# A hybrid mLSTM / gated-DeltaNet layer: the order of a head's work in the mLSTM stage

## Chip, cores, metric

One core of a Trainium2 chip runs the whole program. The metric is device time in microseconds; lower is better. A run of the kernel is compared with runs of the kernel before on the same chip.

## What is computed

One layer of a decoder trunk, for a prompt of 1024 tokens and a group of 8 sequences of 8 sample tokens (1088 tokens in all), float32. All tokens go through one input projection `h @ w_in` (width 1024 in), whose columns feed an mLSTM branch with 4 heads, a gated DeltaNet branch with 8 heads, and gates. Then follow the output projections, a squared-ReLU MLP and a gated side input. The change concerns the mLSTM branch alone. Per head, q and k have 128 columns, v and the output gate 256:

```python
# per chunk; C (128x256) and n (128) are carried
s   = einsum('bhld,bhjd->bhlj', qx, kx) * dw
num = w_inter * einsum('bhld,bhde->bhle', qx, C) + einsum('bhlj,bhje->bhle', s, vx)
nq  = w_inter * einsum('bhld,bhd->bhl', qx, n) + sum(s, axis=-1)
h   = num / maximum(abs(nq), exp(-m_row))
C   = dec * C + einsum('bhl,bhld,bhle->bhde', wk, kx, vx)      # and n likewise
ha  = head_rms(h) * g_norm_a * sigmoid(o_a)
```

The kernel's chunk is 128 tokens: eight of the prompt, and a ninth that holds all 64 sample tokens, each sequence with a C and n of its own, which are read from memory and written back.

## The kernel before

The program runs in stages with a barrier between them: prologue, gates, delta (DeltaNet), mlstm, tail. In each stage every engine has its own program, in order; semaphores join them.

**Projections.** Weights come in slabs of 128 output columns (512 KB). SyncE loads a slab into the one raw buffer (`Weights.load`, L199), VectorE rounds it to the high part (`split_hi`, L209), GpSimd subtracts to get the remainder (`split_lo`, L214), TensorE multiplies in three passes over 8 k-tiles (`product`, L225). High parts and remainders have two buffers. So the load of a slab waits for the remainder of the one before it, and the high part of a slab waits until the products of the slab two before it are done. A slab's product is three groups over tokens (384, 384, 320), each of 24 matmuls into one PSUM bank. A head has six slabs: 0 K, 1 Q, 2 and 3 V, 4 and 5 the output gate. ScalarE copies a group out of its bank (`copy_out`).

**Banks.** `Banks` gives out PSUM banks in a fixed rotation. `claim` makes TensorE wait until the user before has released the bank; six banks serve projections and matrices, two the recurrence, sample states and output transposes.

**A head's other work.** `matrices`: for three thirds of three chunks each, K and V are transposed (L1402) and K·Q formed (L1413). VectorE scales and copies these out and multiplies K·Q by decays; the decays' exponents are made by nine VectorE instructions (L1517) from rows loaded per head, and exponentiated by ScalarE. `scan_all`: for each of eight chunks the state product (L1425), the numerator in two products (L1427, L1429); VectorE updates C (L1547), ScalarE copies the numerator out (L1495). Then the sample numerator (L1435, L1437) and eight sample-state products (L1442), each added to CS by VectorE (L1559) after CS was scaled as a whole (L1555). `finish` on VectorE squares and sums the numerators (L1567 to L1574), ScalarE makes the inverse norm, VectorE scales NUM (L1576), splits slab 2 of the next head, makes the gates (L1582). `outputs`: TensorE transposes NUM (L1451) in six groups of three; VectorE multiplies them with the gates into HT (L1588), which are the buffers V0 and V1.

**Order before.** TensorE: slabs 1 to 5, `matrices`, `scan_all`, slab 0 of the next head, `outputs`. SyncE: for the head before, `stores` (C and n of the prompt, C and n of the samples, both HT tiles to HA; then a wait until the four states have landed); then the decay rows and the new head's CS; then slabs 3, 4, 5 and slabs 0, 1, 2 of the next head. The n stores write single float32 elements. VectorE: splits of slabs 3, 4, 5 and of the next head's 0 and 1, the exponents and `matrices`, `scan_all`, `finish`. ScalarE waits for the HA stores of the head before ahead of its first copy of slab 2.

```python
def turn(h, nxt):                  # TensorE, L1454
    for j in range(1, NJ):
        for g in range(NG):
            group(h, j, g)
    matrices(h)
    scan_all(h)
    if nxt:
        for g in range(NG):
            group(h + 1, 0, g)
    outputs(h)
```

Of the kernel before, what the change touches and what calls it, by code (L numbers as in the profile page):

```python
# [30 lines left out]
NB, NS = 8, 8  # L31
T = SEQ + NB * NS
L = 128
# [43 lines left out]
def wait(eng, ev, turn, n):  # L77
    eng.wait_ge(ev.sem, ev.at(turn, n))
# [151 lines left out]
def build(nc, x_prompt, x_sample, p_prompt, p_sample, state_C, state_n, state_m, state_S, state_conv, g_mix, w_in,  # L230
# [38 lines left out]
    with ctx:  # L269
# [999 lines left out]
        def mlstm():  # L1269
            NJ = 6  # L1270
            E1 = DV_A + 1
            dense = [("dense", j, g) for j in range(NJ) for g in range(NG)]
            mats = [(n, t) for t in range(3) for n in ("kt", "va", "vb", "p")]
            scan = [(n, c) for c in range(NC) for n in ("c", "num")] + [("num", NC)] + [("cs", b) for b in range(NB)]
            turn_ = [(n, t) for t in range(3) for n in ("ta", "tb")]
            B = Banks(psum[0:6], dense + mats, sem, "a_main")
            SB = Banks(psum[6:8], scan + turn_, sem, "a_scan")
            with ExitStack() as st:
# [40 lines left out]
                with nc.Block() as block:  # L1319
                    @block.sync  # L1320
                    def _(sp):
# [4 lines left out]

                        def turn(h, later, nxt):
                            if later:
                                stores(h - 1)
                            for i, (dst, src) in enumerate(((ROW, ROWS_A[bass.ds(h, 1), 0]), (WIN, ROWS_A[bass.ds(h, 1), 1]),  # L1330
                                                            (DECS, DECS_A[bass.ds(h, 1)]))):
                                sp.dma_start(dst[:], src.to_broadcast([P, dst.shape[1]])).then_inc(s_row[i].sem, 16)
                            sp.dma_start(CS[:, :, 0:DV_A], state_C[0, :, bass.ds(h, 1)].rearrange("b a k v -> k (b a) v")).then_inc(s_cs.sem, 16)
                            sp.dma_start(CS[:, :, DV_A:E1], state_n[0, :, bass.ds(h, 1)].rearrange("b a k -> k b a")).then_inc(s_cs.sem, 16)
                            for j in range(3, NJ):
                                slab(h, j)
                            if nxt:
                                for j in range(3):
                                    slab(h + 1, j)
# [48 lines left out]
                    def _(pe):  # L1388
# [15 lines left out]

                        def matrices(h):
                            for t in range(3):
                                turned(h, ("kt", t), K, [("dense", 0, min(t, 2))])
                                turned(h, ("va", t), V0, [("dense", 2, t)])
                                turned(h, ("vb", t), V1, [("dense", 3, t)])
                                bank = B.claim(pe, h, ("p", t), ("dense", 1, t))  # L1410
                                for i in range(3):
                                    a = (3 * t + i) * L
                                    ins = pe.matmul(bank[:, i * L:i * L + L], K[:, a:a + L], Q[:, a:a + L], start=True, stop=True)  # L1413
                                B.filled(ins, ("p", t))

                        def scan_all(h):
                            for c in range(NC):
                                a = c * L
                                if c % 3 == 0:
                                    for n in ("kt", "va", "vb", "p"):  # L1420
                                        B.taken(pe, h, (n, c // 3))
                                if c == 1:
                                    wait(pe, qi, h, 1)
                                bank = SB.claim(pe, h, ("c", c))
                                SB.filled(pe.matmul(bank[:, 0:E1], KW[:, a:a + L], VT[:, c, :], start=True, stop=True), ("c", c))  # L1425
                                bank = SB.claim(pe, h, ("num", c), *([("c", c - 1)] if c else []))
                                ins = pe.matmul(bank[:, 0:E1], ST[:, a:a + L], VT[:, c, :], start=True, stop=(c == 0))  # L1427
                                if c:
                                    ins = pe.matmul(bank[:, 0:E1], Q[:, a:a + L], C[c % 2][:], start=False, stop=True)  # L1429
                                SB.filled(ins, ("num", c))  # L1430
                            a = NC * L
                            bank = SB.claim(pe, h, ("num", NC))
                            wait(pe, s_cs, h, 2)
                            wait(pe, qm, h, 1)
                            pe.matmul(bank[:, 0:E1], ST[:, a:a + L], VT[:, NC, :], start=True, stop=False)  # L1435
                            for b in range(NB):
                                ins = pe.matmul(bank[:, 0:E1], QM[:, P * b:P * b + P], CS[:, b, :], start=False, stop=(b == NB - 1))  # L1437
                            SB.filled(ins, ("num", NC))
                            wait(pe, vm, h, 1)
                            for b in range(NB):  # L1440
                                bank = SB.claim(pe, h, ("cs", b))
                                SB.filled(pe.matmul(bank[:, 0:E1], KW[:, a:a + L], VM[:, b, :], start=True, stop=True), ("cs", b))  # L1442
# [11 lines left out]
                        def turn(h, nxt):  # L1454
                            for j in range(1, NJ):
                                for g in range(NG):
                                    group(h, j, g)
                            matrices(h)
                            scan_all(h)
                            if nxt:  # L1460
                                for g in range(NG):
                                    group(h + 1, 0, g)
                            outputs(h)

                        for g in range(NG):
                            group(0, 0, g)
                        pe.wait_ge(s_init, 6)
# [5 lines left out]
                    def _(act):  # L1473
# [9 lines left out]

                        def turn(h, later):
                            for j in range(NJ):
                                for g in range(NG):
                                    if later and g == 0 and j == 2:
                                        wait(act, s_ha, h - 1, 2)
                                    copy_out(h, j, g)
                            for t in range(3):  # L1490
                                wait(act, dx, h, t + 1)
                                act.activation(third(ST, t), third(ST, t), ACT.Exp).then_inc(dw.sem, 1)
                            for c in range(NCH):
                                src = SB.read(act, h, ("num", c))
                                SB.release(act.activation(NUM[:, c, :], src[:, 0:E1], ACT.Copy), ("num", c))  # L1495

                            wait(act, fin, h, NL - 1)
                            act.activation(rr[:], rr[:], ACT.Ln).then_inc(lnr.sem, 1)
                            wait(act, lnr, h, 1)
                            act.activation(rr[:], rr[:], ACT.Exp, scale=-0.5).then_inc(lnr.sem, 1)  # L1500

                        turn(0, False)
                        with act.Fori(1, H_A) as h:
                            turn(h, True)

                    @block.vector
                    def _(dve):
                        def matrices(h):
                            dve.tensor_copy(HG[:].unsqueeze(1), GTA[:, bass.ds(h, 1)])
# [6 lines left out]
                            for c in range(NCH):  # L1516
                                ins = dve.scalar_tensor_tensor(ST[:, c * L:c * L + L], ROW[:, c * L:c * L + L], HG[:, 0, c:c + 1],  # L1517
                                                               (madd if c < NC else madds)[:], ALU.add, ALU.add)
                                if c % 3 == 2:
                                    ins.then_inc(dx.sem, 1)  # L1520
                            for t in range(3):
                                s = slice(3 * t, 3 * t + 3)
# [13 lines left out]

                        def scan_all(h, later):
                            wait(dve, s_row[2], h, 1)
# [11 lines left out]
                            for t in range(3):  # L1550
                                B.taken(dve, h, ("va", t))
                                B.taken(dve, h, ("vb", t))
                            dve.tensor_tensor(VM[:], over_chunks(VT[:, NC, :], NB), over_tokens(ohb[:], E1), ALU.mult).then_inc(vm.sem, 1)
                            SB.read(dve, h, ("num", NC))
                            dve.tensor_tensor(CS[:], CS[:], over_tokens(DECS[:, NC:16], E1), ALU.mult).then_inc(csd.sem, 1)  # L1555
# [34 lines left out]
                        def turn(h, later, nxt):  # L1590
                            for j in range(3, NJ):
                                WS.split_hi(dve, h, j, B)
                            if nxt:
                                WS.split_hi(dve, h + 1, 0, B)
                                WS.split_hi(dve, h + 1, 1, B)
                            matrices(h)
                            scan_all(h, later)
                            finish(h, nxt)
# [592 lines left out]
```

## Time and profile before

| | |
|---|---|
| Median of 3 runs | 3146.91 us (3145.77 to 3149.1) |
| Profiled execution: time, span | 3151.03 us, 3149.0 us |
| Busy: PE, PEld | 2774.0 us (88%), 2657.4 us (84%) |
| Busy: DVE, ACT, POOL | 1136.8 us (36%), 655.4 (21%), 686.0 (22%) |
| mlstm stage in the span | about 1165 to 1655 us |
| Weight-slab loads of the stage | 24, 512 KB each, 3.9 us to landing (median) |

Times in the views count from the start of the span. PE is TensorE's matmul side and PEld its weight loads; a float32 product appears as two matmuls ("x2"). A row's bracket gives the idle time of the engine ahead of the instruction and what ended it. PEclk is the granted TensorE clock, 1.00 being 2.4 GHz.

### The profile page before, as it was taken

The page shows a single profiled execution, that of the slowest core. Times are in us where ns is not written, and L with a number is a line of the kernel's source. Part 1 is how long each engine was busy: PE and PEld are TensorE (multiplying, and loading weights), DVE is VectorE, ACT ScalarE, POOL GpSimd, SP SyncE. Part 2 cuts the span into 40 slices and gives each one's busy share as a digit, 9 for nine tenths or more (in the row PEclk, how much of TensorE's full clock was granted, in tenths as well). Part 3 has the DMA queues.
Part 4 walks back from the last instruction along what each step waited for, and adds up shares of the span by engine and source line. Part 5 has one row for each costly group of instructions (what it writes and reads, how often), then busy time and mean ns, then how long its engine had stood idle before and what let it go on. Part 6 is the DMA issues. An engine that isn't in the chain of part 4 may idle for free. (4 is left out here: it accounts for less than half of the span.)

```text
span 3149.0 us, 41997 instructions
## 1 busy us (share of the span) xinstructions
PE 2774.0 (88%) x16879; PEld 2657.4 (84%) x16879; DVE 1136.8 (36%) x1791; ACT 655.4 (21%) x1308; POOL 686.0 (22%) x376
## 2 busy tenths in 40 slices
PE   4399889888898879889967998989999999999997
PEld 2388879788787869879857998989999999999987
DVE  2352452533524521442343122154413213223444
ACT  3243443443434421111110000001100001001122
POOL 1330230221202202011003122234211212112422
PEclk7699999999999989999988999999999999999999
DMA  3111111011011112423423121121111111111112
GB/s 118 40 27 51 56 36 49 21 57 56 28 50 50 34 28 76 78 35 83 78 25 107 47 90 43 44 90 47 41 48 41 44 45 41 47 41 41 57 34 75
DMA packets 237643, 165.10 MB, mean 52 GB/s; under 512 B 23755, under 2 KB 225035, under 8 KB 237487
## 3 DMA queue, kind: packets, MB, share of 16 engines
q1 hardware_dynamic: 237542, 163.64, 19.0%
q8 instruction: 77, 1.26, 0.2%
q14 instruction: 24, 0.20, 0.0%
HBM read 135.84 MB, written 27.76 MB: 52 GB/s over the span
## 5 line engine op out<-in xcount | busy, mean ns | idle before, releaser
L214 POOL TENSOR_TENSOR t_w_lo<-t_w_raw,t_w_hi 128x1024 fp32r<-128x1024 f32 x120 | 274.1, 2285 | 1027.3 <-DVE t_w_hi L209 1027.3
L225 PE MATMUL bank<-t_rhi,t_w_lo 128*128 128x384 f32 (+1 forms) x1344 | 444.0, 330 | 40.5 <-POOL t_w_lo L214 20.3
L225 PE MATMUL bank<-hlo,t_w_hi 128*128 128x384 f32 (+1 forms) x1440 | 467.7, 330 | 0.0
L225 PE MATMUL bank<-hhi,t_w_lo 128*128 128x384 f32 (+1 forms) x1344 | 444.1, 330 | 25.8 <-DVE hlo L2060 13.2
L225 PE MATMUL bank<-hhi,t_w_hi 128*128 128x384 f32 (+1 forms) x1344 | 443.7, 330 | 0.0
L225 PE MATMUL bank<-t_rhi,t_w_hi 128*128 128x384 f32 (+1 forms) x1344 | 442.2, 329 | 0.0
L225 PE MATMUL bank<-t_rlo,t_w_hi 128*128 128x384 f32 (+1 forms) x1344 | 442.1, 329 | 0.0
L225 PEld LDWEIGHTS bank<-t_rhi,t_w_lo 128*128 128x128 f32 x1344 | 255.6, 190 | 43.7 <-issue 31.4
L225 PEld LDWEIGHTS bank<-hhi,t_w_lo 128*128 128x128 f32 x1344 | 256.8, 191 | 27.2 <-issue 21.2
L225 PE MATMUL bank<-hhi,b_w_lo 128*128 128x384 f32 (+1 forms) x768 | 262.5, 342 | 16.8 <-POOL b_w_lo L214 12.0
L225 PEld LDWEIGHTS bank<-hlo,t_w_hi 128*128 128x128 f32 x1440 | 274.2, 191 | 0.0
L225 PEld LDWEIGHTS bank<-hhi,t_w_hi 128*128 128x128 f32 x1344 | 256.3, 191 | 0.0
L225 PEld LDWEIGHTS bank<-t_rlo,t_w_hi 128*128 128x128 f32 x1344 | 255.5, 190 | 0.2
L225 PEld LDWEIGHTS bank<-t_rhi,t_w_hi 128*128 128x128 f32 x1344 | 255.4, 190 | 0.0
L225 PE MATMUL bank<-hlo,b_w_hi 128*128 128x384 f32 (+1 forms) x768 | 255.0, 332 | 0.0
L225 PE MATMUL bank<-hhi,b_w_hi 128*128 128x384 f32 (+1 forms) x768 | 254.6, 331 | 0.0
L214 POOL TENSOR_TENSOR b_w_lo<-b_w_raw,b_w_hi 128x1024 fp32r<-128x1024 f32 x32 | 83.8, 2620 | 663.9 <-DVE b_w_hi L209 663.9
L225 PE MATMUL bank<-hhi,a_w_lo 128*128 128x384 f32 (+1 forms) x576 | 192.9, 335 | 11.9 <-POOL a_w_lo L214 11.9
L225 PE MATMUL bank<-hlo,a_w_hi 128*128 128x384 f32 (+1 forms) x576 | 191.4, 332 | 0.0
L225 PE MATMUL bank<-hhi,a_w_hi 128*128 128x384 f32 (+1 forms) x576 | 191.2, 332 | 0.0
L2033 DVE TENSOR_TENSOR t_x<-t_x,bank 128x384 f32<-128x384 f32 (+1 forms) x120 | 63.6, 531 | 339.5 <-PE bank L225 332.2
L1947 ACT ACTIVATE t_acc<-t_v 128x384 f32<-128x384 f32 (+1 forms) x96 | 48.6, 507 | 624.5 <-DVE t_v L2053 624.4
(350 smaller groups left out, 4345.5 us busy)
## 6 DMA issues: line engine op xcount, KB each, us to landing
b_w_raw<-in_w_in_dram SPq DMA_DIRECT2D x32, 512.0 KB, 3.9
t_w_raw<-in_w_up_dram SPq DMA_DIRECT2D x32, 512.0 KB, 3.8
t_w_raw<-in_w_down_dram SPq DMA_DIRECT2D x32, 512.0 KB, 4.0
a_w_raw<-in_w_in_dram SPq DMA_DIRECT2D x24, 512.0 KB, 3.9
t_w_raw<-in_w_in_dram SPq DMA_DIRECT2D x16, 512.0 KB, 3.6
b_gam<-ROWS_B SPq DMA_DIRECT2D x8, 576.0 KB, 4.1
b_eg<-ROWS_B SPq DMA_DIRECT2D x8, 576.0 KB, 5.8
b_kb<-ROWS_B SPq DMA_DIRECT2D x8, 576.0 KB, 6.8
```

The source lines that it names most:

```text
L214: pool.tensor_tensor(self.lo[j % 2][:, 0:kt, :], self.raw[j % self.rs][:, 0:kt, :], self.hi[j % 2][:, 0:kt, :], ALU.subtract).then_inc(sel ...
L225: ins = pe.matmul(out, a[:, k, :], b[:, k, :], start=(start and k == 0 and i == 0), stop=(stop and k == kt - 1 and i == 2))
L1947: act.activation(ACC[:, a:a + w], V[:, a:a + w], ACT.Square).then_inc(rsq.sem, 1)
L2033: B.release(dve.tensor_tensor(XM[:, m, a:a + w], XM[:, m, a:a + w], src[:, 0:w], ALU.add), ("dense", j, g))
```

## The change

TensorE's program is reordered. Slabs 2 and 3 come first in a head's turn; each group of slab 4 is followed by one third of the matrices, each group of slab 5 by two chunks of the recurrence. The next head's slab 0 has its groups between chunks 4-5 and 6-7, behind chunk 7, and behind the sample numerator. The sample states come in two halves with the first group of the next head's slab 1 between them; its other two groups stand ahead of `outputs`. The rotation of the six banks follows that order. ScalarE's copies follow it too. On VectorE the exponents come behind the split of slab 3, the split of the next head's slab 0 behind `matrices`, that of slab 1 inside `scan_all`. On SyncE the load of slab 3 stands ahead of the stores of the head before; slab 4 is now the first load behind them.

```diff
-            dense = [("dense", j, g) for j in range(NJ) for g in range(NG)]
-            mats = [(n, t) for t in range(3) for n in ("kt", "va", "vb", "p")]
+            main = [("dense", j, g) for j in range(4) for g in range(NG)]
+            for t in range(3):
+                main += [("dense", 4, t)] + [(n, t) for n in ("kt", "va", "vb", "p")]
+            main += [("dense", 5, g) for g in range(NG)]
...
-            B = Banks(psum[0:6], dense + mats, sem, "a_main")
+            B = Banks(psum[0:6], main, sem, "a_main")
...
                         def turn(h, later, nxt):
+                            slab(h, 3)
                             if later:
                                 stores(h - 1)
...
-                            for j in range(3, NJ):
+                            for j in range(4, NJ):
                                 slab(h, j)
...
                         def turn(h, nxt):
-                            for j in range(1, NJ):
+                            for j in range(2, 4):
                                 for g in range(NG):
                                     group(h, j, g)
-                            matrices(h)
-                            scan_all(h)
+                            for t in range(3):
+                                group(h, 4, t)
+                                matrices(h, t)
+                            for g in range(NG):
+                                group(h, 5, g)
+                                for c in range(2 * g, 2 * g + 2):
+                                    scan_chunk(h, c)
                             if nxt:
-                                for g in range(NG):
-                                    group(h + 1, 0, g)
+                                group(h + 1, 0, 0)
+                            for c in range(6, NC):
+                                scan_chunk(h, c)
+                            if nxt:
+                                group(h + 1, 0, 1)
+                            sample_out(h)
+                            if nxt:
+                                group(h + 1, 0, 2)
+                            for b0 in (0, NB // 2):
+                                sample_state(h, b0)
+                                if nxt and b0 == 0:
+                                    group(h + 1, 1, 0)
+                            if nxt:
+                                for g in range(1, NG):
+                                    group(h + 1, 1, g)
                             outputs(h)
 
-                        for g in range(NG):
-                            group(0, 0, g)
+                        for j in range(2):
+                            for g in range(NG):
+                                group(0, j, g)
...
                             dve.tensor_tensor(VM[:], over_chunks(VT[:, NC, :], NB), over_tokens(ohb[:], E1), ALU.mult).then_inc(vm.sem, 1)
+                            if nxt:
+                                WS.split_hi(dve, h + 1, 1, B)
                             SB.read(dve, h, ("num", NC))
...
                         def turn(h, later, nxt):
-                            for j in range(3, NJ):
+                            WS.split_hi(dve, h, 3, B)
+                            exponents(h)
+                            for j in range(4, NJ):
                                 WS.split_hi(dve, h, j, B)
+                            matrices(h)
                             if nxt:
                                 WS.split_hi(dve, h + 1, 0, B)
-                                WS.split_hi(dve, h + 1, 1, B)
-                            matrices(h)
-                            scan_all(h, later)
+                            scan_all(h, later, nxt)
                             finish(h, nxt)
```

Left out: `matrices` and `scan_all` of TensorE are cut into `matrices(h, t)`, `scan_chunk(h, c)`, `sample_out(h)` and `sample_state(h, b0)` with the same instructions in each; the first lines of VectorE's `matrices` become `exponents(h)`; ScalarE's `turn` copies groups and numerators in TensorE's new order, with slab 1's last group behind the inverse norm.

## Rows read from the trace of the kernel before

**Rows 1.** Windows of projections: length; busy us (count) of PE, PEld, DVE, ACT, POOL; PEclk; DMA share, GB/s
```profile
1176.01:1190.52 14.51, 14.51 (x73) 14.51 (x74) 0.69 (x1) 0.98 (x2) 3.69 (x7) 0.81 0.58 163
1190.52:1202.52 12.00, 12.00 (x75) 12.00 (x74) 0.69 (x1) 1.42 (x3) 2.40 (x1) 1.00 0.44 122
1304.71:1318.01 13.30, 13.30 (x74) 13.30 (x73) 0.71 (x2) 0.98 (x2) 0.00 (x0) 0.89 0.95 204
```

**Rows 2.** Windows of the matrices: the last head's, and the sum of four
```profile
1597.37:1602.33 4.96, 4.96 (x48) 4.96 (x46) 4.43 (x10) 1.67 (x4) 0.00 (x0) 1.00 0.01 3
sum 36.74, PE 25.67 PEld 24.64 DVE 35.10 ACT 7.69 POOL 7.04; mean PE 6.42 PEld 6.16 DVE 8.77 ACT 1.92 POOL 1.76
```

**Rows 3.** Timeline of PE, head 0: start, us, instruction, count, [idle before <-releaser]
```profile
1256.67 0.69 PE L1402 MATMUL bank<-ident,a_v 128*128 128x128 f32 x2 [3.69 <-DVE a_kw L1524]
...
1264.59 0.60 PE L1429 MATMUL bank<-a_c,a_q 128*128 128x257 f32 x2
1265.03 0.60 PE L1425 MATMUL bank<-a_vt,a_kw 128*128 128x257 f32 x2
...
1266.64 0.60 PE L1425 MATMUL bank<-a_vt,a_kw 128*128 128x257 f32 x2
...
1301.95 2.46 PE L1451 MATMUL bank<-ident,a_num 128*128 128x128 f32 x9 [4.27 <-DVE a_v L1588]
```

**Rows 4.** Windows of the recurrence: the sum of four heads
```profile
sum 55.83, PE 47.33 PEld 32.42 DVE 26.17 ACT 10.79 POOL 0.00; mean PE 11.83 PEld 8.11 DVE 6.54 ACT 2.70 POOL 0.00
```

**Rows 5.** Windows of head 0: sample states, next slab 0, outputs
```profile
1278.60:1284.83 6.23, 4.35 (x17) 2.38 (x16) 4.80 (x8) 1.67 (x2) 0.00 (x0) 1.00 0.00 0
1284.83:1296.86 12.03, 12.03 (x74) 12.00 (x73) 9.24 (x10) 2.46 (x5) 0.00 (x0) 1.00 0.87 82
1296.86:1304.71 7.85, 3.57 (x20) 2.73 (x18) 6.58 (x8) 0.44 (x1) 2.81 (x1) 0.75 0.14 25
```

**Rows 6.** Timeline of SyncE: first state store, n store, row load, slab 3
```profile
1285.39 0.37 SPq L1344 DMA_DIRECT2D out_dram<-a_c  x1
...
1286.96 0.53 SPq L1348 DMA_DIRECT2D out_dram<-a_cs  x1
...
1310.92 0.36 SPq L1332 DMA_DIRECT2D a_row<-ROWS_A  x1
...
1314.15 4.05 SPq L199 DMA_DIRECT2D a_w_raw<-in_w_in_dram  x1
```

**Rows 7.** DMA issues of three heads' ends: KB, us to landing (n store; slab 3)
```profile
a_w_raw<-in_w_in_dram SPq DMA_DIRECT2D x1, 512.0 KB, 9.2
...
out_dram<-a_cs SPq DMA_DIRECT2D x1, 4.0 KB, 23.8
...
out_dram<-a_cs SPq DMA_DIRECT2D x1, 4.0 KB, 21.5
...
out_dram<-a_cs SPq DMA_DIRECT2D x1, 4.0 KB, 26.0
```

**Rows 8.** Timeline of DVE, end of head 0
```profile
1283.57 0.86 DVE L1559 TENSOR_TENSOR a_cs<-a_cs,bank 128x257 f32<-128x257 f32 x2 [0.36 <-PE bank L1442]
1284.78 0.86 DVE L1559 TENSOR_TENSOR a_cs<-a_cs,bank 128x257 f32<-128x257 f32 x2 [0.36 <-PE bank L1442]
1285.56 2.55 DVE L1567 TENSOR_TENSOR a_sqn<-a_num 128x2304 f32<-128x2304 f32 x1
...
1293.40 2.56 DVE L1576 TENSOR_TENSOR a_num<-a_num,a_rr 128x2304 f32<-128x2304 f32 x1 [1.67 <-ACT a_rr L1500]
1297.13 0.69 DVE L209 CAST a_w_hi<-a_w_raw 128x1024 fp32r<-128x1024 f32 x1 [1.17 <-PE bank L225]
1297.74 3.56 DVE L1582 TENSOR_SCALAR a_o<-a_o,a_gh 128x1088 f32<-128x1088 f32 x2
```

**Rows 9.** Timeline of POOL: remainders of slabs 2 and 3 of head 1
```profile
1297.90 2.81 POOL L214 TENSOR_TENSOR a_w_lo<-a_w_raw,a_w_hi 128x1024 fp32r<-128x1024 f32 x1 [44.00 <-DVE a_w_hi L209]
1324.21 2.40 POOL L214 TENSOR_TENSOR a_w_lo<-a_w_raw,a_w_hi 128x1024 fp32r<-128x1024 f32 x1 [23.49 <-DVE a_w_hi L209]
```

More of the change, by code:

```diff
@@ L1403, in turned @@
                             B.filled(ins, slot)
[L1405 to L1430, printed above, removed]
+                        def matrices(h, t):
+                            turned(h, ("kt", t), K, [("dense", 0, min(t, 2))])
+                            turned(h, ("va", t), V0, [("dense", 2, t)])
+                            turned(h, ("vb", t), V1, [("dense", 3, t)])
+                            bank = B.claim(pe, h, ("p", t), ("dense", 1, t))
+                            for i in range(3):
+                                a = (3 * t + i) * L
+                                ins = pe.matmul(bank[:, i * L:i * L + L], K[:, a:a + L], Q[:, a:a + L], start=True, stop=True)
+                            B.filled(ins, ("p", t))
@@ new lines, in scan_chunk @@
+                        def scan_chunk(h, c):
+                            a = c * L
+                            if c % 3 == 0:
+                                for n in ("kt", "va", "vb", "p"):
+                                    B.taken(pe, h, (n, c // 3))
+                            if c == 1:
+                                wait(pe, qi, h, 1)
+                            bank = SB.claim(pe, h, ("c", c))
+                            SB.filled(pe.matmul(bank[:, 0:E1], KW[:, a:a + L], VT[:, c, :], start=True, stop=True), ("c", c))
+                            bank = SB.claim(pe, h, ("num", c), *([("c", c - 1)] if c else []))
+                            ins = pe.matmul(bank[:, 0:E1], ST[:, a:a + L], VT[:, c, :], start=True, stop=(c == 0))
+                            if c:
+                                ins = pe.matmul(bank[:, 0:E1], Q[:, a:a + L], C[c % 2][:], start=False, stop=True)
+                            SB.filled(ins, ("num", c))
@@ L1431, in scan_all, with sample_out @@
+                        def sample_out(h):
                             a = NC * L
@@ L1438, in scan_all, with sample_state @@
                             SB.filled(ins, ("num", NC))
+                        def sample_state(h, b0):
+                            a = NC * L
                             wait(pe, vm, h, 1)
-                            for b in range(NB):
+                            for b in range(b0, b0 + NB // 2):
                                 bank = SB.claim(pe, h, ("cs", b))
@@ L1482, in copy_out, with numerator, turn @@
                             B.release(ins, ("dense", j, g))
-                        def turn(h, later):
-                            for j in range(NJ):
+                        def numerator(h, c):
+                            src = SB.read(act, h, ("num", c))
+                            SB.release(act.activation(NUM[:, c, :], src[:, 0:E1], ACT.Copy), ("num", c))
+                        def turn(h, later, nxt):
+                            for j in range(2, 4):
                                 for g in range(NG):
@@ L1492, in turn @@
                                 act.activation(third(ST, t), third(ST, t), ACT.Exp).then_inc(dw.sem, 1)
-                            for c in range(NCH):
-                                src = SB.read(act, h, ("num", c))
-                                SB.release(act.activation(NUM[:, c, :], src[:, 0:E1], ACT.Copy), ("num", c))
+                            for g in range(NG):
+                                copy_out(h, 4, g)
+                            for g in range(NG):
+                                copy_out(h, 5, g)
+                                for c in range(2 * g, 2 * g + 2):
+                                    numerator(h, c)
+                            if nxt:
+                                copy_out(h + 1, 0, 0)
+                            for c in range(6, NC):
+                                numerator(h, c)
+                            if nxt:
+                                copy_out(h + 1, 0, 1)
+                            numerator(h, NC)
+                            if nxt:
+                                copy_out(h + 1, 0, 2)
+                                for g in range(2):
+                                    copy_out(h + 1, 1, g)
                             wait(act, fin, h, NL - 1)
@@ L1500, in turn, with exponents @@
                             act.activation(rr[:], rr[:], ACT.Exp, scale=-0.5).then_inc(lnr.sem, 1)
-                        turn(0, False)
-                        with act.Fori(1, H_A) as h:
-                            turn(h, True)
+                            if nxt:
+                                copy_out(h + 1, 1, 2)
+                        for j in range(2):
+                            for g in range(NG):
+                                copy_out(0, j, g)
+                        turn(0, False, True)
+                        with act.Fori(1, H_A - 1) as h:
+                            turn(h, True, True)
+                        turn(H_A - 1, True, False)
                     @block.vector
                     def _(dve):
-                        def matrices(h):
+                        def exponents(h):
                             dve.tensor_copy(HG[:].unsqueeze(1), GTA[:, bass.ds(h, 1)])
@@ L1520, in matrices @@
                                     ins.then_inc(dx.sem, 1)
+                        def matrices(h):
                             for t in range(3):
@@ L1535, in matrices, with scan_all @@
                             dve.tensor_copy(QM[:].rearrange("p (b x) -> p b x", x=P + NS)[:, :, 0:NS], sequences(Q)).then_inc(qm.sem, 1)
-                        def scan_all(h, later):
+                        def scan_all(h, later, nxt):
                             wait(dve, s_row[2], h, 1)
@@ L1553, in scan_all @@
                             dve.tensor_tensor(VM[:], over_chunks(VT[:, NC, :], NB), over_tokens(ohb[:], E1), ALU.mult).then_inc(vm.sem, 1)
+                            if nxt:
+                                WS.split_hi(dve, h + 1, 1, B)
                             SB.read(dve, h, ("num", NC))
```

## The prediction

> **What bounds the kernel now.** The page comes first, with the table above: TensorE (PE) is busy for most of the span, and nothing else for much over a third, so time moves only where the matrix engine waits, runs at half its clock, or is made to. Next come the stretches of the mLSTM stage. A head has six slabs of projections, 12.00 us each at full clock [rows 1], and behind slab 5 stand four pieces with little to cover their waits. (1) Transposes and K·Q products, "matrices": 36.74 us over four heads, of which the last, whose exponents were ready, takes 4.96 [rows 2]. The other three share 31.78: each has a wait of 3.69 for a VectorE (DVE) product [rows 3]. (2) The recurrence over eight chunks: 55.83 over four heads, TensorE modelled busy for 47.33 [rows 4]. (3) The sample states, 6.23 [rows 5] (first of three, within 0.1 of each other). (4) The outputs, 7.85 (first of three, likewise), at granted clock 0.75 (1.00 is 2.4 GHz, 0.5 is 1.2), with one wait of 4.27 for VectorE [rows 3, 5]. The reader should see that these are latencies between engines, not work.
>
> Then the quiet side, SyncE's program. It issues in order; its store routine ends in a wait until a head's states have landed, and the next head's row loads stand behind it. The stores begin at 1285.39, the row loads can only go at 1310.92 [rows 6], because the 4 KB store of n (4 bytes a packet) takes 23.8 us to land; 21.5 and 26.0 at the next heads [rows 7]. Today this hides behind three slabs.
>
> I call E the end of a head's last sample product (1284.83), H the moment at which NUM is scaled (1293.40 + 2.56 = 1295.96), O the end of the output transposes (1304.71) [rows 5, 8].
>
> **Part by part.** The instructions are the same in kind and number; order and bank rotation change.
>
> *Matrices.* Each third now has a slab-4 group in front, and the exponents are taken behind slab 3's split, long before. The nearest row is the last head's 4.96, with its exponents early. Saved: 31.78 − 3 × 4.96 = 16.9 us (bounds: 5.8, if a wait of 3.69 stays in each of three heads, to 16.9).
>
> *Recurrence.* A chunk takes 1.61 (1265.03 to 1266.64); a product without a wait takes 0.44 (1264.59 to 1265.03) [rows 3], so three make 1.31, and the 23 of a head 10.0. The other 0.3 is the wait for ScalarE's copy of the numerator before. Behind a projection group the first chunk of a pair does not pay it and the second does: 4 × 0.3 stay, and 0.3 at the first copy of C. That is 11.5 a head, and 12.1 in the last, where chunks 4 to 7 stand together. Saved: 55.83 − 3 × 11.5 − 12.1 = 9.2 (bounds 6 to 13).
>
> *Sample states.* CS is scaled under a group of the next head's slab 0 and no longer in TensorE's way. What is left is VectorE's pace of additions, 1.21 for two [rows 8], behind a first pair at 0.9: 2.1 for each half of four, 4.2 against 6.3. Saved three times: 6.3 (bounds 4 to 7.5).
>
> *Outputs.* Here cover is lost. H ends a chain on VectorE that begins 0.73 behind E: squares, sum, norms, scaling, to E+11.1 [rows 8]. Before, the 12.03 of slab 0 stood there [rows 5]; now only two groups of slab 1 (704 of 1088 columns of 12.00: 7.8). TensorE waits 3.3 for H, turns six blocks, and waits again while VectorE splits slab 2 and makes the gates (0.69 and 3.56). Before, O was H+8.75, 1.17 of it an idle VectorE in wait for slab 0 [rows 8]; that goes, so O = H+7.6 = E+18.7. Outputs outside the projections: 18.7 − 7.8 = 10.9 against 7.85. Lost: 3 × 3.1 = 9.3 (bounds 6 to 15, by how long the half clock lasts).
>
> These four alone give −16.9 − 9.2 − 6.3 + 9.3 = **−23.1 us**.
>
> *SyncE's queue.* Slab 3's load moves ahead of the stores, and it waits until slab 2's remainder is made, which is split only behind H. Split 0.69, remainder 2.81 [rows 8, 9]: slab 3 is issued at H+3.6 = O−4.0. The stores begin at O−3.4, about 15 us later in the head than before (E+0.56), and the n store goes 1.57 behind the first [rows 6], at O−1.8. At 23.8 it lands at O+22.0. Then the row loads go; slab 4, now behind them, is issued 3.2 later (1310.92 to 1314.15) and takes 9.2 [rows 6, 7]: landed at O+34.4. Split and remainder end 3.3 behind that (1314.15 + 9.2 against 1324.21 + 2.40 [rows 9]): O+37.7. The exponents, also behind the rows, are made while slab 4 is in flight and add nothing.
> TensorE has only slabs 2 and 3 to do before slab 4 (slab 1 is already done): 24.0, and 1.3 for the half clock behind the outputs (13.30 against 12.00 [rows 1]), so it is ready at O+25.3. **It waits 12.4 us in front of slab 4, in heads 1 to 3**; in head 0 there are no stores and no wait. It restarts at half clock: the stage's first slab, behind the stage's first long wait, took 14.51 against 12.00 [rows 1], 2.5 more. Lost: 3 × (12.4 + 2.5) = 44.7. Before, slab 3 was the one behind the stores: its remainder was there at 1326.6 and TensorE wanted it at 1304.71 + 13.30 + 12.00 = 1330.0, so this path was 3.4 us from the end already.
> Bounds: with n at 21.5 and slab 4 two us sooner behind emptier queues the wait is 8; with n at 26.0, the slab-3 load in front of the stores and both HA stores close behind, it is 20.
>
> Two waits look dangerous and aren't. ScalarE waits for the HA stores at slab 2, near O+26, but six banks let TensorE finish slab 3. The splits of the next head's slabs 0 and 1, now behind matrices and recurrence, still come several us ahead of their use.
>
> *A rule against this.* For the n store the row shows 23.8 us for 1,024 elements of 4 bytes [rows 7]. The Trainium skill, DMA: Bandwidth & Descriptors, section Bandwidth (Measured), gives a 4 KB transfer 0.68 us, about 10.5 ns a packet. By that price of the Trainium skill, an estimate, the stores would be down long before slab 4 is wanted, and the sum would be −23 us. Its table is of loads into SBUF; this trace's stores into memory disagree in every head, and I go by the trace.
>
> **The sum.** −23.1 + 44.7 = **+21.6 us**. The profiled execution took 3151.03 with a span of 3149.0, and is 4.1 over the median of 3146.91. The same terms give 3172.6 for it and **3168.5 us** for the time to be measured.
>
> **The rivals.**
> A. *The stores drain sooner.* If a store begun at O−3.4 is down by O+9, slab 4 is in time and only the first four terms stay: −23.1, 3124 us. A wait of 3 that is left gives −23.1 + 3 × 5.5 = −6.6, 3140, and is of this case too. For it: 4 KB is little, and what holds it up is not seen. Against: three heads between 21.5 and 26.0.
> B. *A wash.* The wait in front of slab 4 is some 5 us: −23.1 + 3 × 7.5 = −0.6, 3146 us. The change turns sign at a wait of 5.2.
> C. *A larger stall.* Slab 3's load and HA share the queues with the states, and the wait is 20: −23.1 + 3 × 22.5 = +44.4, 3191 us.
> D. *It does not do what it says.* TensorE still stands at the matrices, on a bank or on late exponents, and 11.1 of the 16.9 stay lost: with the stall +32.7, 3180. It is in the forecast's upper side.
>
> **How the numbers follow.** Forecast (waits of 8 to 16, D among them): 0.63, its own range 3152 to 3182. A 0.15, B 0.09, C 0.13. A measurement here tells 0.2%, 6.3 us, from no change. Faster is A and a little of B: 0.17. Same is most of B and the forecast's low tail: 0.10. Slower: 0.73. The range that leaves out two in ten is 3145 to 3192.
>
> **What would show it.** In the profile after: an idle of about 12 us in front of slab 4's first matmul in heads 1 to 3, put down to POOL's a_w_lo, none in head 0; row loads issued about 22 us behind the output transposes; half clock just behind. Matrices outside the projections at about 5 us a head; 0.3 us waits at every second chunk only; an idle of 3 us for the scaled NUM and one of 4 for a_v at the outputs. I am wrong if slab 4 starts right behind slab 3 (A), or if the idle there is far from 12 (B, C).

## The result and the profile after

The changed kernel takes **3162.87 us** (median of 5, 3160.46 to 3167.17) against 3146.91 before (median of 5, 3143.63 to 3149.54): ratio 1.0053, 95% interval 1.0038 to 1.0067, 16.0 us slower. The forecast was 3168.5, 21.6 slower, in a range of 3145 to 3192.

The spans of the two profiled executions are cut at the first and the last product of the mLSTM stage. First before, then after (columns as in [rows 1]).

```profile
0.00:1176.01 1176.01, 949.37 (x6227) 873.30 (x6227) 477.10 (x759) 456.31 (x943) 255.11 (x196) 0.93 0.15 46
1176.01:1644.10 468.09, 416.73 (x2300) 386.07 (x2300) 166.68 (x258) 65.32 (x136) 57.59 (x29) 0.94 0.31 63
1644.10:3149.00 1504.90, 1407.94 (x8353) 1398.05 (x8352) 493.00 (x774) 133.75 (x229) 373.31 (x153) 0.96 0.18 54
```

```profile
0.00:1177.57 1177.57, 956.15 (x6228) 879.10 (x6228) 477.38 (x759) 456.68 (x943) 255.30 (x196) 0.92 0.15 46
1177.57:1663.05 485.48, 409.52 (x2300) 383.95 (x2300) 161.23 (x258) 64.06 (x136) 57.42 (x29) 0.91 0.35 60
1663.05:3161.20 1498.15, 1399.77 (x8353) 1389.39 (x8352) 493.57 (x774) 133.95 (x229) 373.61 (x153) 0.97 0.18 54
```

The stage is 17.4 us longer, though TensorE is busy 7.2 us less in it. The stages around it, the same code, differ by 5.2 us the other way in this pair, so the two spans differ by 12.2. (The profiled execution of the kernel before is 4.1 above its median, that of the changed kernel is its median: hence 16.0 between the medians.)

The pieces outside the projections, as sums over windows: the matrices of head 0 (three thirds), its recurrence (four pairs), its sample states (two halves), and the outputs of heads 0 to 2 beyond the last projection group. They answer to [rows 2, 4, 5].

```profile
sum 4.71, PE 4.71 PEld 4.71 DVE 3.14 ACT 1.42 POOL 0.00; mean PE 1.57 PEld 1.57 DVE 1.05 ACT 0.47 POOL 0.00
sum 10.55, PE 10.27 PEld 7.56 DVE 4.10 ACT 3.46 POOL 1.20; mean PE 2.57 PEld 1.89 DVE 1.02 ACT 0.86 POOL 0.30
sum 3.86, PE 3.63 PEld 2.45 DVE 1.73 ACT 0.93 POOL 0.00; mean PE 1.81 PEld 1.23 DVE 0.86 ACT 0.46 POOL 0.00
sum 32.29, PE 12.02 PEld 8.92 DVE 27.15 ACT 2.73 POOL 8.44; mean PE 4.01 PEld 2.97 DVE 9.05 ACT 0.91 POOL 2.81
```

In the first three PE is busy nearly throughout: the waits between engines are gone. In the fourth it works 12.02 of 32.29. The idle times on PE's timeline show why, and what is new: two waits at the outputs of head 0, then one in front of slab 4 in heads 1, 2 and 3.

```profile
1302.79 1.54 PE L1457 MATMUL bank<-ident,a_num 128*128 128x128 f32 x6 [3.23 <-DVE a_num L1629]
1307.38 0.90 PE L1457 MATMUL bank<-ident,a_num 128*128 128x128 f32 x3 [3.06 <-DVE a_v L1641]
...
1346.69 0.68 PE L225 MATMUL bank<-hhi,a_w_lo 128*128 128x384 f32 x1 [11.35 <-POOL a_w_lo L214]
...
1469.51 0.68 PE L225 MATMUL bank<-hhi,a_w_lo 128*128 128x384 f32 x1 [14.01 <-POOL a_w_lo L214]
...
1593.44 0.69 PE L225 MATMUL bank<-hhi,a_w_lo 128*128 128x384 f32 x1 [15.44 <-POOL a_w_lo L214]
```

GpSimd, which the brackets name, is only the last link: it makes the remainder as soon as the slab is there. SyncE's timeline behind head 0 shows where the slab was held: slab 3 at 1306.36, the first store behind it, the n store, then 22.6 us with nothing but HA's stores, the row load, and slab 4. Before, the first store stood at 1285.39 [rows 6].

```profile
1306.36 0.38 SPq L199 DMA_DIRECT2D a_w_raw<-in_w_in_dram  x1
1307.03 0.37 SPq L1347 DMA_DIRECT2D out_dram<-a_c  x1
...
1308.61 0.67 SPq L1351 DMA_DIRECT2D out_dram<-a_cs  x1
...
1331.26 0.36 SPq L1335 DMA_DIRECT2D a_row<-ROWS_A  x1
...
1334.13 4.10 SPq L199 DMA_DIRECT2D a_w_raw<-in_w_in_dram  x1
```

The DMA issues behind heads 0, 1 and 2 give the n store's time to landing (last column). It takes about as long as before (21.5 to 26.0 [rows 7]), only later in the head. SyncE's wait is for all four state stores, and this one is the last of them.

```profile
out_dram<-a_cs SPq DMA_DIRECT2D x1, 4.0 KB, 22.5
...
out_dram<-a_cs SPq DMA_DIRECT2D x1, 4.0 KB, 24.2
...
out_dram<-a_cs SPq DMA_DIRECT2D x1, 4.0 KB, 25.3
```

TensorE restarts below full clock. The rows are the first group of slab 4 in heads 1, 2 and 3, with a mean granted clock of 0.73, 0.73 and 0.59; the full-clock time is 4.24 (12.00 × 384/1088).

```profile
1346.69:1352.41 5.72, 5.72 (x25) 5.69 (x26) 0.69 (x1) 0.00 (x0) 1.00 (x1) 0.73 0.34 92
1469.51:1475.25 5.74, 5.74 (x25) 5.71 (x26) 0.69 (x1) 0.00 (x0) 0.98 (x1) 0.73 0.35 91
1593.44:1600.23 6.79, 6.79 (x24) 6.77 (x25) 0.69 (x1) 0.00 (x0) 2.23 (x1) 0.59 0.30 80
```

### The profile page after: what moved, and what is told of

Its sections match the earlier page's. It is cut to its first block and busy times, and to the rows that moved or that the text cites. A ratio compares the mean times of both kernels' runs of the same rounds, so it can differ in the third digit from the quotient of the medians.

```text
span 3161.2 us, 41991 instructions
## 1 busy us (share of the span) xinstructions
PE 2765.4 (87%) x16879; PEld 2652.4 (84%) x16879; DVE 1132.2 (36%) x1791; ACT 654.7 (21%) x1308; POOL 686.3 (22%) x376
```

## The experiments

Theory: the new order of TensorE is a gain; all of the loss is the wait of slab 4 behind the state stores. Rivals: the late stores cost by themselves; VectorE's new order makes the slab late; the landing time is that of 1 MB, not of the single elements. Runs e1 to e4 were on one chip (the kernel before took 3147.04 there), e5 to e8 on another (3145.93); each ratio is to the kernel before on the same chip.

**e1: SyncE's order of before, all else changed.**

```diff
-                            slab(h, 3)
                             if later:
                                 stores(h - 1)
...
-                            for j in range(4, NJ):
+                            for j in range(3, NJ):
                                 slab(h, j)
```

> The changed kernel with SyncE's order of before: stores of the head before, row and CS loads, then slabs 3, 4, 5. Theory (the place of slab loads behind the state stores sets the end): the stores begin at E+0.5 again, the rows go at E+26, and now slab 3 is the load behind them: issued E+29, landed E+38, remainder E+41.5, while TensorE wants it at O+13.3 = E+32. So the wait moves from slab 4 to slab 3 and shrinks from 11 to 15 us down to about 9.5: 3 x (9.5 + 2) in place of the 46 us now lost in waits and half clock, about 3151 us. Rival (the wait comes from the reordered splits or exponents on VectorE, not from SyncE's queue): the wait stays in front of slab 4 and near 12, 3163.

Measured: 3152.26, ratio 1.0020 (1.0011 to 1.0029). The wait moved to slab 3 and is 8.56, 7.18 and 10.38 us in heads 1 to 3; head 1's, on PE's timeline:

```profile
1333.01 0.69 PE L225 MATMUL bank<-hhi,a_w_lo 128*128 128x384 f32 x1 [8.56 <-POOL a_w_lo L214]
```

The slab that stands behind the stores is the slab that is late, whichever it is. VectorE's order is that of the change, and slab 4 no longer waits, so VectorE's order is not what made it late.

**e2: the state stores first, then slab 3, then HA.** `stores` is cut into `states` (the four state stores) and `outs` (HA and the wait).

```diff
+                            if later:
+                                states(h - 1)
                             slab(h, 3)
                             if later:
-                                stores(h - 1)
+                                outs(h - 1)
```

> The changed kernel with SyncE's order: state stores of the head before, slab 3, HA stores, the wait, rows and CS, slab 4. Theory: state stores begin at E+0.5 and are down at about E+25, O+6.5; slab 3 is issued at O-4 and may land with them, still ahead of its use at O+13; rows go at O+6.7, slab 4 lands at O+19.5 and its remainder is there at O+23, just ahead of O+25. No wait in front of a slab is left, and the 46 us of waits and half clock go: 3117 us, 30 below the kernel before. Rival A (a load behind the element-wise stores is held up beyond their end, or holds them up): slab 3 late by some us per head, 3125 to 3140. Rival B (something else on VectorE is next, the exponents): a wait of 5 stays in front of slab 4, 3133.

Measured: **3117.86**, ratio 0.9915 (0.9901 to 0.9928), 29 us below the kernel before. In heads 1 to 3 slab 4 never waits, and slab 3 once, 0.17 us in head 3. So the whole loss was in the queue; with it out of the way the reordering of TensorE is worth 29 us. The DMA issues behind head 0 show a side effect:

```profile
out_dram<-a_cs SPq DMA_DIRECT2D x1, 1024.0 KB, 15.6
a_w_raw<-in_w_in_dram SPq DMA_DIRECT2D x1, 512.0 KB, 12.7
...
out_dram<-a_cs SPq DMA_DIRECT2D x1, 4.0 KB, 23.1
```

Slab 3, issued at 1305.24, 12.5 us behind the n store, needs 12.7 us where a slab has 3.9 (median), and lands 2 us behind the n store. The Trainium skill (DMA: Bandwidth & Descriptors, Queues, rings and completion order) says that a semaphore increment lands only after every earlier write of its DMA engine. This trace can't tell whether that increment is held, but it shows that more is at work. These are the packets of four windows: 1301.5 to 1302.8, to 1306, to 1315.5, to 1318.

```profile
DMA packets 1239, 0.19 MB, mean 147 GB/s; under 512 B 1056, under 2 KB 1239, under 8 KB 1239
DMA packets 0, 0.00 MB, mean 0 GB/s; under 512 B 0, under 2 KB 0, under 8 KB 0
DMA packets 655, 0.34 MB, mean 35 GB/s; under 512 B 0, under 2 KB 655, under 8 KB 655
DMA packets 496, 0.66 MB, mean 265 GB/s; under 512 B 18, under 2 KB 387, under 8 KB 496
```

The n store's 1,024 packets are on record by 1302.8, yet it lands at 1315.88, 13 us later. Slab 3's packets (512 B each) begin at 1306 and pass at 35 GB/s until about that moment, then fast. So the slab is not kept from starting, and its increment alone is not what is late: its own data move slowly while the n store is out.

**e3: the kernel before with SyncE's new order alone.** The reverse of e1's edit, put on the kernel before.

> The kernel before with only SyncE's new order (slab 3 ahead of the stores). Theory: slab 4's remainder comes at O+38 to O+41, and TensorE, with slabs 1 to 3 to do behind the outputs, wants it at O+37.3: the same late stores cost only 0.5 to 4 us a head, 3147 to 3158, likely 3151. The loss needs both, the late stores and the slab of work taken out from behind the outputs. Rival (late stores cost by themselves): a wait of 12 per head here too, 3185.

Measured: 3147.96, ratio 0.9999 (0.9990 to 1.0008): no change. The GpSimd row is slab 4's remainder of head 1, done at 1341.89; the output transposes ended at 1307.3, so TensorE wanted it three slabs later (13.30 + 12.00 + 12.00), at 1344.6.

```profile
1339.49 2.40 POOL L214 TENSOR_TENSOR a_w_lo<-a_w_raw,a_w_hi 128x1024 fp32r<-128x1024 f32 x1 [15.51 <-DVE a_w_hi L209]
```

Heads 2 and 3 have no wait in front of a slab either. So the late stores cost nothing by themselves, in head 1 by 2.7 us of slack. It takes slab 1's 12 us out from behind the outputs to make a wait. With the stores early (e1) that wait is 26.1 us over three heads, with them late (the change) 40.8.

**e4: the changed kernel without the two n stores** (n of prompt and samples isn't written, and the wait counts two stores).

```diff
-                            sp.dma_start(n_prompt[0, 0, bass.ds(h, 1)].rearrange("a k -> k a"), c[:, DV_A:E1]).then_inc(s_st.sem, 16)
...
-                            sp.dma_start(n_sample[0, :, bass.ds(h, 1)].rearrange("b a k -> k b a"), CS[:, :, DV_A:E1]).then_inc(s_st.sem, 16)
```

> The changed kernel without the two stores of n per head (128 and 1024 single elements); those outputs are not written. Theory (the element-wise stores make the landing long): C of the samples, 1 MB in rows of 1 KB, lands in 6 to 9 us, rows go at about O+6, slab 4 is there at O+22, no wait: 3117 us. Rival (the 1 MB store itself, or the queue, is slow): C of the samples still takes 15 to 19 us as it does with n in the queue, the wait in front of slab 4 shrinks by 4 to 6 us a head only, 3146 to 3150.

Measured: 3111.24, ratio 0.9886 (0.9871 to 0.9901), and no wait in front of a slab in heads 1 to 3. C of the samples lands in 5.9 us behind head 0; with n it took 19.0 there, and 17.5 to 19.3 behind heads 0 to 2.

```profile
out_dram<-a_cs SPq DMA_DIRECT2D x1, 1024.0 KB, 5.9
```

The stores of a head count up one semaphore, so the landing of one also hangs on those ahead of it. But the bytes moved tell the same. In the changed kernel, from 1306 on in slices of 0.75 us, slab 3 and the 1 MB pass at up to 375 GB/s, then the 1 MB falls to 7 to 75 GB/s for some 5 us before its rest goes through:

```profile
GB/s 0 8 114 235 352 348 375 175 31 7 25 15 23 56 75 190 268 168 29 29 29 17 29 52 23 35 41 52 86 64 133 145 151 261 128 313 240 203 277 270
```

It is the 1,152 single elements that make the landing long, and they hold up the 1 MB beside them. The expected 3117 was 6 us too high. That difference to e2 lies at the stage's end, where the last head's stores are waited for: from the last output product to the first product of the next stage it is 12.2 us here and 17.9 in e2.

**e5 to e7: what bounds e2.** e5 moves VectorE's gate products from behind the scaled NUM to ahead of the sample numerator; e6 puts the two halves of the sample states together and the whole of slab 1 behind them; e7 does both. Left out below: the same lines taken out of `finish`, and ScalarE's copies, which follow TensorE's order.

```diff
+                        def gates(h):
+                            step(h, 1, dve.tensor_scalar(GH[:], GH[:], float(DV_A) ** 0.5, None, ALU.mult))
...
+                                ins = dve.tensor_scalar(OG[i][:], OG[i][:], 1.0, GH[:, i:i + 1], ALU.add, ALU.mult)
...
+                            gates(h)
                             SB.read(dve, h, ("num", NC))
```

```diff
                                 sample_state(h, b0)
-                                if nxt and b0 == 0:
-                                    group(h + 1, 1, 0)
                             if nxt:
-                                for g in range(1, NG):
+                                for g in range(NG):
```

> e2 with VectorE's gate products (two of 1.8 us, and the scaling of GH) moved from behind the scaled NUM to in front of the sample numerator, where VectorE waits. Theory: the second wait of the outputs (3.1 to 3.8 us a head) goes, and TensorE reaches slab 3 that much sooner; but slab 3, held up by the element-wise n stores, has its remainder only at E+31, where TensorE now wants it at about E+29: 2 us of the gain come back as a wait there. Net some 1.5 to 3 us a head: 3110 to 3114. Rival (the stores are no bound there any more): the full 3.4 us a head and the half clock, 3105.

> e2 with both halves of the sample states together and all three groups of the next slab 1 between them and the output transposes (ScalarE's copies ordered to suit). Theory: TensorE no longer stands 3.2 us for the scaled NUM, since 12.0 us of groups cover the chain of 11.1; the states, without a group between, cost 0.5 us more. 3 x 3 us and a little half clock less: 3107. Rival (the end of the outputs is set by VectorE's chain, and slab 3 by the stores, so the time is only moved): 3115 to 3118.

> e5 and e6 together, on e2's queue. Theory: the outputs cost 3.3 us, no wait but the pace of VectorE; slab 3, whose landing is tied to the n stores at E+27.5, is wanted at E+27.6 and there at E+31: a wait of 3.2 in front of slab 3 in heads 1 to 3 eats the gates' gain, about 3106, 1 below e6. Rival (no such tie): 3095.

Measured: e5 3114.48 (0.9900, 0.9885 to 0.9916), e6 3107.76 (0.9875, 0.9860 to 0.9891), e7 3106.98 (0.9875, 0.9860 to 0.9890). More cover is a clear gain over e2. The gates alone, and on top of e6, bring nothing that is clear of the noise: the intervals overlap. In e5 the waits of the outputs for the gated buffers fall from 10.7 us to 0.6 over the stage, and the waits in front of slab 3 rise from 0.2 to 7.2. PE's timeline at head 1's slab 3, in e5 and in e7 (2.98, 1.60 and 2.38 in its three heads):

```profile
1320.50 0.45 PE L225 MATMUL bank<-hhi,a_w_lo 128*128 128x384 f32 x1 [2.45 <-POOL a_w_lo L214]
```

```profile
1316.30 0.44 PE L225 MATMUL bank<-hhi,a_w_lo 128*128 128x384 f32 x1 [2.98 <-POOL a_w_lo L214]
```

**e8: e7 with the queue rebuilt.** The edit is shown against e7. At a head's end only the two C stores; the row loads at once, since nothing of the old head reads ROW, WIN or DECS any more; the element-wise stores behind slab 4; and the wait only ahead of what it guards, the loads of CS.

```diff
                                 states(h - 1)
-                            slab(h, 3)
-                            if later:
-                                outs(h - 1)
...
+                            slab(h, 3)
+                            if later:
+                                outs(h - 1)
+                            slab(h, 4)
+                            if later:
+                                norms(h - 1)
+                            slab(h, 5)
+                            if later:
+                                wait(sp, s_st, h - 1, 4)
...
-                            for j in range(4, NJ):
-                                slab(h, j)
```

> e7 with SyncE's queue rebuilt: at a head's end only the two C stores, then the row loads of the next head, slab 3, HA, slab 4, then the two n stores, slab 5, the wait for all stores, the loads of CS, slabs 0 to 2. Theory: no slab load that is wanted soon has an element-wise store ahead of it; slab 5, held up to about E+42, is wanted at E+56. No wait in front of any slab: 3093, 54 below the kernel before. Rival A (slab 5 or the loads behind it are late): a wait of some 5 us a head at slab 5, 3108. Rival B (row loads and C stores ahead of slab 3 hold it up): 3100.

Measured: **3096.45**, ratio 0.9840 (0.9827 to 0.9854), 49.5 us below the kernel before and about 66 below the change; 3093 was expected. The stage is 417.16 us long, 10.1 shorter than in e7: e7's three waits in front of slab 3 (7.0) and the low clock behind two of them (3.2) are gone. The edit moves the n stores, the row loads, the wait and the loads of CS together, and no run tells how much each of them is worth. The stage's weight matmuls, grouped by line, have one wait left, that for the stage's first slab; the same row of the changed kernel stands below it.

```profile
L225 PE MATMUL bank<-hhi,a_w_lo 128*128 128x384 f32 (+1 forms) x576 | 195.2, 339 | 11.8 <-POOL a_w_lo L214 11.8
```

```profile
L225 PE MATMUL bank<-hhi,a_w_lo 128*128 128x384 f32 (+1 forms) x576 | 199.1, 346 | 53.0 <-POOL a_w_lo L214 53.0
```

## Why the prediction was right, step by step

- *Matrices.* 4.71 in head 0, and 18.84 over four heads against 36.74: 17.9 saved, forecast 16.9.
- *Recurrence.* 10.55, twice 10.49 and 11.35: 42.9 against 55.83, 12.9 saved, forecast 9.2, the term furthest off. A pair takes 2.72, not 2.9: the wait in it is 0.1, and the first copy of C costs 0.15. Part goes back: a 384-column group between pieces takes 4.43 where 4.24 was reckoned, some 4 us over all heads.
- *Sample states.* 3.86 in head 0 against 6.23; 11.4 against 18.9 over three heads, 7.4 saved, forecast 6.3.
- *Outputs.* 10.78, 10.76 and 10.75 against 7.85, forecast 10.9. The two waits are 3.23 and 3.06 (3.81 in the later heads), where 3.3 and about 4 were said. Lost 8.7, forecast 9.3.
- *SyncE's queue.* Slab 3 is issued at O−3.8, the n store at O−1.6, the rows go at O+21.1 and slab 4 at O+24.0 (O = 1310.18); forecast O−4.0, O−1.8, O+22.0, O+25.2. Slab 4 then takes 9.2 to 9.4 us to land, forecast 9.2. The state stores are down by then, but 2.2 MB of rows and CS are issued in the 2.9 us ahead of it; a slab without them takes 3.9, so part of the delay is theirs. The waits are 11.35, 14.01 and 15.44, in sum 40.8 for a forecast of 37.2. No wait in head 0.
- *The half clock behind it.* Sized too high. About 1.5, 1.5 and 2.6 us, 5.5 in all, where 3 × 2.5 was taken from the stage's start; only in head 3 did the half clock last as long as there.

The terms as measured make −17.9 − 12.9 − 7.4 + 8.7 + 40.8 + 5.5 + 4 = +20.8; the stage shows +17.4. Most of the rest is a gain that the forecast left out. Behind the outputs it reckoned 1.3 us of low clock before and after the change alike. The first projection group behind them takes, summed over heads 1 to 3, first before, then after:

```profile
sum 17.18, PE 17.18 PEld 17.18 DVE 2.14 ACT 0.00 POOL 0.00; mean PE 5.73 PEld 5.73 DVE 0.71 ACT 0.00 POOL 0.00
sum 14.61, PE 14.61 PEld 14.61 DVE 4.53 ACT 0.00 POOL 7.21; mean PE 4.87 PEld 4.87 DVE 1.51 ACT 0.00 POOL 2.40
```

That is 2.6 us. Three sample numerators, 3.7 against 3.9 each, give 0.6 more, and 0.2 us stay unassigned.

The mechanism came as forecast: which slab waits, behind what, and for how long. That the sum is off by only 5.6 us is in part luck. The first four terms gained 6.4 us more than was said, the low clock cost 2.0 less, and the 3.2 above weren't in the sum; against them stand 3.6 us more of waits and 4 of longer groups. The first four terms, forecast as −23.1, are −29.5; e2, where nothing waits for the queue, measures −29. Rival A, the stores draining sooner, fails on the three landings of 22.5 to 25.3; its time of 3124 is 6 us above what the kernel does once they are out of the way (e2), and the −23 us of the rule against the forecast did not come either. Rival B's 5 us and C's 20 did not come, and D fails on the matrices.

## What to carry to other kernels

When work is moved to fill the waits of one engine, the distance between two other events shrinks; list what was hidden in that distance. Here it was the queue of loads behind a wait for stores, with 3.4 us to spare. SyncE issues in order, so a wait belongs directly ahead of what it guards, and slow element-wise stores belong where no load that is wanted soon stands behind them. The same reordering of TensorE cost 16 us or gained 29 by the place of the stores and one load in the queue alone; with more cover, the gates moved and the queue rebuilt it gained 49.

## What the runs showed of the hardware that was not expected

- A 1 MB store with rows of 1 KB lands behind heads 0 to 2 in 5.9 to 6.2 us without the single-element stores (e4), and with 128 such writes ahead of it and 1,024 behind it in 17.5 to 19.3 (the change) or 13.7 to 15.6 (e2).
- The 1,024 single elements (4 KB) take 21.5 to 26.0 us to land there in the kernel before, 22.5 to 25.3 in the change and 21.5 to 25.0 in e2. In e2 their packets are on record 13 us before the landing behind head 0.
- A 512 KB load issued 12.5 to 12.8 us behind them lands after 11.6 to 14.6 us (e2), 2 to 3 us behind them, in place of 3.9. Behind head 0 its packets pass at 35 GB/s while they are out.
